# A fused transformer block: two opening modulation chunks moved to TensorE, and the other chunks moved inside the feed-forward bodies

## The reference, cut to what matters

```python
c_act = jax.nn.silu(c)                                  # 1 x 1024
for i in range(2):
    mod = c_act @ mod_w[i] + mod_b[i]                   # 1024 x 9216: nine vectors of 1024
    sh1, sc1, g1, sh2, sc2, g2, sh3, sc3, g3 = jnp.split(mod, 9, axis=-1)
    h = modulate(rmsnorm(x, norm_g[i, 0]), sh1, sc1)    # h * (1 + scale) + shift
    x = x + 0.5 * g1 * swiglu(h, w13[i, 0], w2[i, 0])   # hidden width 2816
    h = modulate(rmsnorm(x, norm_g[i, 1]), sh2, sc2)
    x = x + g2 * mixer_i(h)                             # layer 0: pool and SSD; layer 1: MLA attention
    h = modulate(rmsnorm(x, norm_g[i, 2]), sh3, sc3)
    x = x + 0.5 * g3 * swiglu(h, w13[i, 1], w2[i, 1])
```

## Time and profile before

| | |
|---|---|
| median of 3 runs | 1763.58 us (1763.45 to 1764.44) |
| span of the profiled execution | 1764.7 us |
| PE matmul busy | 1669.9 us, 95% |
| DVE busy | 1290.2 us, 73% |
| ACT busy | 933.4 us, 53% |
| mean DMA rate | 200 GB/s |

### The profile page before, as it was taken

One profiled execution on the slowest core, in us unless ns is written; L12 is line 12 of the kernel. 1 busy time (PEld: TensorE's weight loads), 2 busy tenths in 40 slices (PEclk: granted clock), 3 DMA queues, 4 the chain that ended last, 5 costly groups with the idle time before them and its releaser, 6 DMA issues.

```text
span 1764.7 us, 31956 instructions
## 1 busy us (share of the span) xinstructions
PE 1669.9 (95%) x11230; PEld 1500.6 (85%) x11230; DVE 1290.2 (73%) x2161; ACT 933.4 (53%) x1664; POOL 86.6 (5%) x151
## 2 busy tenths in 40 slices
PE   6899999999999999999999999999988899999998
PEld 5899989888999889998777888898976789988886
DVE  6888888768888888876566666679888565456665
ACT  1544457644444544445575555555467845555553
POOL 2000010300000100000000000000000000000000
PEclk9999999999999999999999999999999999999999
DMA  8888866757888888865433766444633155446561
GB/s 348 311 295 297 306 173 204 156 203 249 300 292 307 236 293 302 294 184 175 131 108 70 240 191 185 148 148 151 186 97 91 49 191 168 143 136 198 191 184 65
DMA packets 123657, 352.76 MB, mean 200 GB/s; under 512 B 9851, under 2 KB 52875, under 8 KB 114225
## 3 DMA queue, kind: packets, MB, share of 16 engines
q1 hardware_dynamic: 108128, 262.18, 46.4%
q10 hardware_dynamic: 12432, 78.65, 13.8%
q0 software_dynamic: 3008, 10.74, 1.9%
HBM read 347.31 MB, written 4.22 MB: 199 GB/s over the span
## 4 chain that ended last, share of the span: by engine, by line
PE 55%; DVE 20%; issue 11%; ACT 8%; DMA 4%; ACTq 1%; POOL 1%; DVEq 0%; POOLq 0%; SPq 0%
PE ps L829 36%; PE ps L1062 8%; PE ps L1063 4%; DVE w_lo L195 4%; DVE arena L358 4%; DVE arena L2680 2%; ACT w_hi L1116 2%; ACT w_hi L189 2%; DVE w_lo L1127 1%; DMA gate_scratch<-gcol 1%; DMA resid<-in_x 1%; DVE resid L1322 1%; DVE act_s L1196 1%; DMA grow<-gate_scratch 1%; ACTq L332 1%
## 5 line engine op out<-in xcount | busy, mean ns | idle before, releaser
L829 PE MATMUL ps<-t_both,w_hi 128*128 128x256 f32 x3952 | 725.9, 285 | 10.1 <-DVE t_both L758 5.7
L829 PEld LDWEIGHTS ps<-t_both,w_hi 128*128 128x128 f32 x3952 | 615.0, 191 | 23.5 <-issue 10.6
L829 PE MATMUL ps<-t_both,w_lo 128*128 128x256 f32 x1976 | 558.5, 283 | 1.3 <-issue 1.3
L195 DVE TENSOR_TENSOR w_lo<-raw,w_hi 128x1024 fp32r<-128x1024 f32 x240 | 288.6, 1222 | 122.6 <-ACT w_hi L189 122.4
L829 PEld LDWEIGHTS ps<-t_both,w_lo 128*128 128x128 f32 x1976 | 376.6, 191 | 0.2
L1127 DVE TENSOR_TENSOR w_lo<-raw,w_hi 128x1024 fp32r<-128x1024 f32 x258 | 313.6, 1221 | 83.0 <-ACT w_hi L1116 82.9
L1116 ACT ACTIVATE w_hi<-raw 128x1024 fp32r<-128x1024 f32 x258 | 268.8, 1053 | 120.2 <-PE ps L829 79.2
L189 ACT ACTIVATE w_hi<-raw 128x1024 fp32r<-128x1024 f32 x240 | 248.2, 1053 | 143.1 <-PE ps L829 99.6
L1062 PE MATMUL ps<-t_both,w_hi 128*128 128x512 f32 x640 | 226.7, 398 | 0.0
L829 PE MATMUL ps<-w_hi,g_hi 128*128 128x512 f32 x440 | 176.8, 402 | 14.4 <-DVE g_lo L1199 11.9
L1063 PE MATMUL ps<-t_both,w_lo 128*128 128x256 f32 x640 | 179.7, 281 | 0.0
(11 more groups left out here) (378 smaller groups left out, 1662.4 us busy)
## 6 DMA issues: line engine op xcount, KB each, us to landing
raw<-in_stream SPq DMA_DIRECT2D x498, 512.0 KB, 4.5
arena<-in_mod_w ACTq DMA_DIRECT2D x72, 1024.0 KB, 7.2
grow<-gate_scratch POOLq DMA_DIRECT2D x6, 512.0 KB, 7.7
u_scratch<-u_keep ACTq DMA_DIRECT2D x1, 3072.0 KB, 36.8
arena<-u_scratch POOLq DMA_DIRECT2D x8, 256.0 KB, 3.3
small<-in_small POOLq DMA_DIRECT2D x1, 1368.0 KB, 11.2
resid<-in_x POOLq DMA_DIRECT2D x1, 1024.0 KB, 18.9
arena<-in_mem POOLq DMA_DIRECT2D x1, 1024.0 KB, 5.4
```

The costliest lines, as they stand in the source:

```text
L195: VE.tensor_tensor(w_lo[:, s, :], raw[:, s, :], w_hi[:, s, :].bitcast(F32), ALU.subtract).then_inc(lo_done, 1)
L829: last = TE.matmul(out, lhs, rhs, start=start and i == 0, stop=stop and i == 2)
```

## The change

It has four parts.

1. **Opening.** SP first loads `c` alone and holds the weight stream until chunk 2 has landed; POOL loads x, the constants and the one-hots only once half of chunk 1 has landed. DVE makes chunks 0 and 2. PE makes chunks 1 and 3 by `mod_columns`: 32 matmuls a chunk with a 128x128 tile of the modulation weights as stationary operand and one column of `cact` as moving operand. The two `keep_busy` calls and the thirty bias matmuls leave the opening.
2. **Boundaries.** `late_mod`, its turn and `mod_add` are gone. Chunk 14 (and in calls 1 and 2 the chunk of the last body) is made wholly in the last body, fold included. Chunk 15 has its eight products and its fold in the output product of the mixer. `mod_finish` (gather, take, place) comes behind the next narrow product, or in the mixer before the last group of the output product.
3. **First bodies.** Calls 1 and 2 make their chunks in bodies 1 to 10, none in body 0. Call 2 therefore has chunks in bodies 9 and 10, where it had none.
4. **Bias products.** They run in the norms ahead of call 2 and ahead of the MLA mixer, 15 matmuls in each, in place of `keep_busy(7)`; ACT copies the results.

```diff
 @block.sync
+    sp.dma_start(col("c", 0, 8), a["cols"][:, COL["c"][0]:COL["c"][1]]).then_inc(c_in.sem, c_in.up(16))
     for s in range(RING):
-        if s == 2:
-            sp.wait_ge(mod_landed[0][1], 32)
+        if s == 0:
+            sp.wait_ge(mod_landed[2][1], 16)
         sp.dma_start(raw[:, s, :], a["stream"][s, :, :]).then_inc(landed[s], 16)
...
+def mod_columns(pe, c):
+    for half in range(2):
+        pe.wait_ge(mod_landed[mod_pair(c)][half], mod_landings(c))
+    for j in range(4):
+        at = 32 * (4 * c + j)
+        for k in range(KT):
+            last = TE.matmul(ps[7][:, at:at + 1], mraw[mod_pair(c)][k // 4][:, k % 4, j * P:(j + 1) * P],
+                             cact[:, k:k + 1], start=k == 0, stop=k == KT - 1)
+    last.then_inc(mod_cols, 1)
...
 @block.tensor
-    pe.wait_ge(first_in.sem, first_in.n)
-    pe.wait_ge(inputs.sem, inputs.n)
+    pe.wait_ge(A.sem, silu_at)
+    mod_columns(pe, 1)
+    pe.wait_ge(first_in.sem, first_in.n)
     mod_turn(pe, 0, first=True)
-    mod_turn(pe, 1, first=True)
-    keep_busy(ps[4], 8)
+    mod_columns(pe, 3)
     mod_turn(pe, 2, first=True)
-    keep_busy(ps[4], 6)
-    mod_turn(pe, 3, first=True)
+    TE.matmul(ps[0][0:16, 0:384], relx, oh[:, 0:384], start=True, stop=True).then_inc(T.sem, T.up())
...
 def dve_body(dve, i, static, mod):
-        closing = t == 1 and static and i == FG - 1
-        if mod is not None and not opening and not closing:
+        if mod is not None and not opening:
             mod_products(dve, mod, range(4 * t, 4 * t + 2), turns)
...
-    if mod is not None and not (late and late_mod):
+    if mod is not None:
         mod_fold(dve, mod, turns)
...
-ffn(1, FG, PRE + FG + 1, (mod_at(0, 8), 0.5), next_mod=PRE + 2 * FG + 1)
+ffn(1, range(1, FG), PRE + FG + 1, (mod_at(0, 8), 0.5), load_on=True)
-norm_x(..., (mod_at(1, 0), mod_at(1, 1)), late_mod=PRE + 2 * FG, late_load=True, busy=7)
+norm_x(..., (mod_at(1, 0), mod_at(1, 1)), filler=lambda pe: bias_products(pe, 0))
-ffn(2, N_MOD - PRE - 2 * FG - 1, PRE + 2 * FG + 1, (mod_at(1, 2), 0.5))
+ffn(2, range(1, FG), PRE + 2 * FG, (mod_at(1, 2), 0.5))
```

More of the change, by code:

```diff
@@ L393, in mod_take @@
                 rows = slice(32 * g, 32 * g + 32)
-                last = E.activation(mod_sum[rows, :], ps[7][rows, g:16:4], ACT.Copy)
+                last = E.activation(mod_sum[rows, :], ps[7][rows, place + g:place + 16:4], ACT.Copy)
             last.then_inc(mod_taken, 1)
@@ L417, in _ @@
                     mod_load(act, half, c)
-            act.wait_ge(first_in.sem, first_in.n)
+            act.wait_ge(c_in.sem, c_in.n)
             E.activation(cact[:, :], col("c", 0, 8), ACT.Silu).then_inc(A.sem, A.up())
+            for half in range(2):
+                mod_load(act, half, 3)
         silu_at = A.n
@@ new lines, in bias_products, with bias_keep, _ @@
+        def bias_products(pe, q):
+            pe.wait_ge(distance_in.sem, distance_in.n)
+            if q:
+                pe.wait_ge(A.sem, bias_kept[q - 1])
+            for n in range(N_CMP):
+                d0 = 256 + q * P - (16 * n + 31)
+                last = TE.matmul(ps[6][:, L + n * 16:L + (n + 1) * 16], ohd[:, d0:d0 + P], relx[0:32, :], start=True, stop=True)
+            last.then_inc(T.sem, T.up())
+            bias_at[q] = T.n
+        def bias_keep(q):
+            @block.scalar
+            def _(act):
+                act.wait_ge(T.sem, bias_at[q])
+                E.activation(biasc[:, q, 0:N_CMP, :], ps[6][:, L:L + N_CMP * 16].rearrange("p (n h) -> p n h", h=16),
+                             ACT.Copy).then_inc(A.sem, A.up())
+            bias_kept[q] = A.n
@@ L534, in _, with squares @@
             for half in range(2):
-                mod_load(act, half, PRE, extra=8 * PRE)
+                mod_load(act, half, PRE)
+        @block.gpsimd
+        def _(pool):
+            pool.wait_ge(mod_landed[1][1], 32)
+            pool.dma_start(small[:, :], a["small"]).then_inc(small_in.sem, small_in.up(16))
         rstd_diag = ar(XN - 256, QT, P)
         junk = ar(XN, 2 * QT, 512)
-        turns_at = {PRE + FG - 1: PRE, PRE + FG: PRE + 1, PRE + 2 * FG: PRE + 2}
-        def squares(src, ready, late_mod=None):
+        def squares(src, ready):
             pooled, rooted, diag_at = {}, {}, {}
@@ L674, in _ @@
                         keep_busy(ps[4], busy)
+                        if filler is not None:
+                            filler(pe)
                         pe.wait_ge(A.sem, entry[1])
@@ L1017, in _, with ffn @@
                     mod_load(act, half, c)
[L1020 removed]
+        def ffn(call, mod_bodies, mod0, residual, load_on=False):
             h0 = blocks["pe"]
@@ L1027, in ffn @@
             fresh = turned["at"] == (V.n, A.n)
-            late_mod = n_mod == FG
-            wide = n_mod == 0
+            wide = not mod_bodies
             sb0 = 2 * (FG - 1) * (call - 3)
-            turns = (PRE, PRE + 2, PRE + 3, None, None)[call]
+            turns = PRE
             def slot(j):
@@ L1204, in dve_body @@
                         mod_products(dve, mod, range(4 * t, 4 * t + 4), turns)
-                    if mod is not None and closing:
-                        mod_products(dve, mod, range(4 * t, 4 * t + 2), turns)
-                    elif mod is not None and t == 1 and not opening:
+                    if mod is not None and t == 1 and not opening:
                         mod_products(dve, mod, range(4 * t + 2, 4 * t + 4), turns)
@@ L1325, in _, with norm_x @@
                         x_ready[q, f] = V.n
-        def norm_x(gain, mods=None, ready=None, mods_before=0, early=4, late_mod=None, late_load=False, busy=0,
-                   after_squares=None):
+        def norm_x(gain, mods=None, ready=None, mods_before=0, early=4, busy=0,
+                   after_squares=None, filler=None):
             if mods is not None:
```

251 lines of the change are left out of this document (118 added, 133 removed).

## The result

The changed kernel takes 1778.67 us (median of 4 runs, 1773.73 to 1780.31) beside 1763.86 us of the kernel before in the same job: a ratio of 1.0071, 95% interval 1.0058 to 1.0083, 15 us or 0.7% slower. I had forecast 1770 and a range up to 1776. The direction was right, the size was not.

The account below looks back on a forecast made before the run. It took TensorE (95% busy) as the main bound, but not in the opening, with DVE alone working at boundaries. Terms of +5.45 plus 1.2 for the clock took the span from 1764.7 to 1771.35, forecast 1770 us, range 1758 to 1776.

Parts of the forecast that it names:

- Opening, +7.3: Start of the kernel: two chunks on PE at 0.215 us a record and a slow first feed-forward start, +7.3 us.
- Rival A: Opening: the one-column matmuls reach the fast pace, opening -2.5 us instead of +7.3, total 1759 us; chance 0.20.
- First bodies, -5.0 and -4.9: Calls 1 and 2: without a chunk in body 0 DVE has more time, saving 5.0 and 4.9 us.
- Rival B: Calls 1 and 2: the first bodies' gain goes to later bodies, half the gain, total 1775 us; chance 0.12.
- rival C: Calls 1 and 2: bodies with a chunk keep 17.2 us, giving 2.5 us more, total 1767.5 us; chance 0.09.
- Behind call 0, +2.1: Boundary behind call 0: added DVE products and fold make the residual start 2.3 us later, net +2.1 us.
- First mixer, +2.5: End of the first mixer: PE waits 2.4 to 3.1 us at its gather for DVE's fold, net +2.5 us.
- Behind calls 1 and 2, +1.35 and +1.8: Boundaries behind calls 1 and 2: as behind call 0, less because the gate row lands near the residual's start.
- 0.6 each for the clock: Two norms with bias products: narrow matmuls may leave a start at half clock, 0 to +1.7 us, taken as +0.6 each.
- The rival, that it is the clock whatever the order: After the result, for the unforecast loss: TensorE's clock causes it, not DVE's order and the bias products; no chance given.
- The base: Whole kernel: the median was put 1.1 us below the span, turning 1771.35 us into 1770.
- rival D: Half clocks after the mixer's gather and in both norms, 4.6 us in place of 1.2, total 1773.6 us; chance 0.09.

Follow-up runs that it names:

- fold_behind: Changed kernel with last bodies cut short on DVE: two products behind the residual, the fold split behind the diagonal and the norm; ratio 1.0051.
- open_fill: Changed kernel with twelve 128-wide fillers between the turn of chunk 0 and the columns of chunk 3 in the opening; ratio 1.0116.
- order_back: Changed kernel with the products for k = 4 and 5 of each last body behind the second hidden tile's gating, as before; ratio 1.0063.
- old_open: Changed kernel with the opening of before: four chunks on DVE, bias products in the opening, seven wide fillers in both norms; ratio 1.0025.
- bias_out: Changed kernel with the fifteen bias products of each norm replaced by six wide fillers and one 256-column matmul, bias not computed; ratio 1.0071.
- fixed_after: Changed kernel with all edits of best3 at boundaries and in the mixer, its own opening and bias products kept; ratio 1.0039.
- best3: best1 with the fold's reduction ahead of the weight splits, gate row requested one body earlier, mixer's gather between the norm's transposes; 1761.13 us, ratio 0.9972.
- mix_late: Changed kernel with only chunk 15's gather, copy and bias addition moved into the norm behind the first mixer; ratio 1.0068.
- open_mix: Changed kernel with four 128-wide fillers behind every eight one-column matmuls of chunk 3 in the opening; ratio 1.0125.
- rows_form: Changed kernel with chunks 1 and 3 made with 512 weight columns moving against one stationary column, eight matmuls a chunk; ratio 1.0035.
- best1: Changed kernel with the old opening and bias products, the short last bodies of fold_behind, and the first mixer's products and fold one block earlier; ratio 1.0019.

## Why the prediction was right in sign and wrong in size

**Opening, +7.3: right,** +7.53, in part by luck. The chosen end of the one unknown price, 0.215 us a record, was measured at 0.215. The start of chunk 3 at 31 was not: the chunk had landed 1.7 us earlier, and the wait for the bias columns, which no term had, made up for it. The five other traces with this opening have +6.0 to +7.3. Rival A did not come: the granted clock prints 1.00 in such a stretch, and only the pace of the records tells. The rule of the Trainium skill, "TensorE: Matmul & The Clock Gate", section "Part 1: The HAM clock gate", that sustained matmul activity releases the throttle, did not describe 13.8 us of uninterrupted one-column matmuls.

**First bodies, -5.0 and -4.9: right,** -5.36 and -4.74, and bodies 0 and 1 of call 1 took 34.05 to 34.07 us in all thirteen kernels that had the edit. Rival B and rival C did not come.

**Behind call 0, +2.1: right,** +1.96, by the mechanism given: the residual slipped by 2.5 us (2.3 forecast), and fold_behind took it away. That the sum came out so close is luck too: six other traces with the same code there have +1.8 to +4.5, and in the three above +3 the products waited 0.65 to 2.14 us for their chunk, as behind calls 1 and 2.

**First mixer, +2.5: the wait was right (2.4 to 3.1 forecast, 2.67 measured), the sum too large:** +1.12, since 1.26 us of idle "issue" time was gone. With the same mixer code other traces have +1.1 to +3.1; of the four at about +2.7 or more, three have a half-clock stretch behind the gather and one (open_fill) again an idle "issue" time, of 1.59 us.

**Behind calls 1 and 2, +1.35 and +1.8 with 0.6 each for the clock: here it failed.** Measured +6.82 and +5.08. The step that failed is the one that took the boundary behind call 0 and then subtracted, because "the gate row lands there about when the residual starts". The gate row did land at about that time in the kernel before (595.30 beside 595.42 in call 1; in call 2 the residual waited 2.17 us for it), but it bounded nothing any more: the residual slipped by 3.38 and 2.88 us (18.93 against 15.55, 18.51 against 15.63 into the last body), and the gate row had landed 1.8 and 5.0 us ahead of it. The second term that failed is that of the bias products, priced at nothing "while they end before the transposes": they did not end before them. The runs show the parts:

```
                residual's start,    from it to the     from it to the
                into the last body   first transpose    first matmul
behind call        1      2             1      2           1      2
before           15.55  15.63          5.48   5.47       10.94  10.43
after            18.93  18.51          7.63   6.49       14.38  12.63
order_back       18.09  18.09          5.48   5.47       12.19  12.23
old_open         19.12  18.64          5.48   5.47       11.68  11.11
bias_out         19.92  18.77          6.05   5.47       10.65  10.41
fixed_after      15.04  15.08          6.52   7.35       12.74  14.14
best3            15.04  15.94          5.48   5.48       10.83  10.87
```

*The residual.* The fold and the two products more are DVE work on the path: 2.5 us in order_back, where nothing waits for a landing. The rest comes from the wait of the two products ahead of the gating for the chunk's second half, 1.44 us in call 1 and 1.01 in call 2: I had moved them in DVE's order without asking when their data lands there. *The transposes.* They started 2.15 and 1.0 us late behind the bias products, which followed a last group that was itself late. At full pace the thirty records take 3.6 us; in the changed kernel behind call 1 they took 4.50, part of them at half clock. Where PE was done earlier (order_back) they delayed nothing. *The clock.* In 17 of the 18 norms with bias products, over nine kernels, a half-clock stretch began behind the residual's start; of the ten behind calls 1 and 2 without them only three had one, each behind a PE wait of 2.2 us or more. With the transposes on time, one such stretch costs up to some 0.8 us (11.59 to 11.68 in six kernels against 10.83 in best3): the 0.6 each that I took was near. The rival, that it is the clock whatever the order, is refuted as the whole: in order_back the clock was full up to the residual, which was still 2.5 us late, and with the order of best3 the residual is early.

**The base, too:** I put the median 1.1 us below a span. The profiled execution of after took 1.75 us more than its span; if that of before did too, it stands at about 1766.5, some 2.6 us over its own median. The difference of the two traces is 11.75 us, that of the medians 14.8; the prediction would have been low by those 3 us even with every term right. My rival D had the direction of the clock's share and 1773.6 us, too little as well; no half clock stood behind the mixer's gather in this trace.

What stays open: how much of +6.82 belongs to that one execution. With the same code at that place the other traces have +3.83 to +5.00 behind call 1, and +3.5 to +8.5 behind call 2.

## What to carry to other kernels

Work moved in an in-order queue takes its data's landing time with it: before an operation is put ahead of a critical one, look up when its transfer lands in that stage, and not only how long it runs. A removed wait uncovers the next (here the fold's reduction, then the gate row, then the gather), so follow the residual's start in microseconds from a fixed point, edit by edit; it told more than the time, which in three of the runs (order_back, bias_out, mix_late) moved by less than its interval. Work on a matmul engine that nothing needs yet is only free if it ends before the first matmul that it stands ahead of could start, at the lower of the two clocks, and if it leaves the clock as it was. And one trace is one execution: the same code gave +1.8 to +4.5 us behind call 0, so a term that is hit to 0.1 us in a single trace is not yet confirmed to 0.1 us.

## What the runs showed of the hardware that I had not expected

PE could be busy without a gap for long and stay at half pace. One-column and 16-column records against 128 stationary columns stayed at 0.215 us for 13 us in the opening; with eight 128-wide records for every sixteen of them they stayed there for 20 us (open_mix). Twenty-four 128-wide records in a row were followed by the full clock, and it fell back to a granted 0.50 under one-column matmuls without any idle gap (open_fill). Under records with a 512-wide moving operand against a single stationary column it rose as well (rows_form).

The length of a wait did not tell by itself what the clock did after it. Behind wide matmuls the transposes stayed at full clock after waits of 2.24 us (call 0 of the changed kernel) and 2.29 us (best1, call 2), and were followed by a half-clock stretch after 2.26 us (old_open, call 2). Behind the thirty 16-column bias records one followed waits of 0.35 to 0.39 us (both norms of open_mix, call 1 of rows_form) and 1.90 us (order_back), where best3's waits of 0.77 and 0.51 us behind wide fillers left the transposes at 0.13 us a record. And a granted clock that prints 1.00 need not mean full pace: between 31 and 44 us it prints 1.00 in the changed kernel, while the records stand 0.215 us apart.
